# The first half of the tokens goes through all of stage B before the second half's output projection, and gets its u and z by seven block products

## The reference

```python
# mixer A
p = h @ w_in                                  # 1024 -> 3 x 1024
a, g_glu, z = split(p)
c = a * sigmoid(g_glu)
y = causal_dwconv(concat([hist, c]))          # 31 taps, channel by channel
y = silu(layernorm(y)) * silu(z)
x = x + rmsnorm(y @ w_out)                    # 1024 -> 1024
# mixer B
p = h @ w_in                                  # 1024 -> u, v, z of 2048 each
u, v = split(gelu(p[:2 * 2048])) ; z = p[2 * 2048:]
v = layernorm(v)
mixed = einsum('gij,bcjgd->bcigd', w_s, v) + bias   # w_s 128x128 for each group, block-causal
s = (u * mixed) * silu(z)
x = x + rmsnorm(s @ w_out)                    # 2048 -> 1024
```

## Time and profile before

| | |
|---|---|
| median of three runs | 2355.88 us (2352.59 to 2357.32) |
| the profiled execution | 2360.95 us, span 2359.2 us |
| TensorE's mean granted clock | 0.992 of full speed |
| busy: TensorE, VectorE, ScalarE, GpSimd | 98%, 64%, 36%, 10% of the span |
| bytes over the span | 265.20 MB, mean 112 GB/s |

### The profile page before, as it was taken

One profiled execution on the slowest core, in us unless ns is written; L12 is line 12 of the kernel. 1 busy time (PEld: TensorE's weight loads), 2 busy tenths in 40 slices (PEclk: granted clock), 3 DMA queues, 4 the chain that ended last, 5 costly groups with the idle time before them and its releaser, 6 DMA issues.

```text
span 2359.2 us, 29993 instructions
## 1 busy us (share of the span) xinstructions
PE 2303.3 (98%) x12208; PEld 2009.2 (85%) x12208; DVE 1507.5 (64%) x1913; ACT 845.5 (36%) x1329; POOL 243.8 (10%) x419
## 2 busy tenths in 40 slices
PE   7899999999999999999999999999999998999998
PEld 6788899999888888888877878879999997888885
DVE  5589889887578988888735852277766766222121
ACT  5422223223353214343544542226566665111110
POOL 1100000010221110000001211111000000100000
PEclk9999999999999999999999999999999999999999
DMA  4323333322544313333442442213333236232220
GB/s 164 124 89 100 106 118 136 109 102 92 166 165 166 114 69 94 106 114 104 141 153 98 144 153 94 83 45 93 103 98 101 96 102 243 107 107 98 82 93 23
DMA packets 118441, 265.20 MB, mean 112 GB/s; under 512 B 16288, under 2 KB 52384, under 8 KB 116256
## 3 DMA queue, kind: packets, MB, share of 16 engines
q1 hardware_dynamic: 94816, 184.64, 24.1%
q0 software_dynamic: 23488, 78.64, 8.8%
HBM read 184.86 MB, written 78.75 MB: 112 GB/s over the span
## 4 chain that ended last, share of the span: by engine, by line
PE 95%; DMA 1%; DVE 1%; ACT 1%; issue 1%; POOL 0%; SPq 0%; ACTq 0%; DVEq 0%
PE PS L1879 30%; PE PS L1880 30%; PE PS L1881 30%; PE PS L2083 1%; PE PS L2111 1%; PE PS L1925 1%; PE PS L1947 1%; PE PS L1890 1%; DMA raw<-wa_in_in 0%; DMA zb<-silu_z_scratch 0%; PE PS L1934 0%; DMA xt<-x_in 0%; DVE xn L1322 0%; PE PS L2113 0%; ACT xn L951 0%
## 5 line engine op out<-in xcount | busy, mean ns | idle before, releaser
L1351 DVE SCALAR_TENSOR_TENSOR acc<-cp,cw,acc 128x513 f32<-128x513 f32 (+3 forms) x464 | 360.4, 777 | 13.9
L1879 PE MATMUL PS<-HAh,Wh 128*128 128x512 f32 (+2 forms) x960 | 342.0, 356 | 0.1
L1880 PE MATMUL PS<-HAl,Wh 128*128 128x512 f32 (+2 forms) x960 | 340.1, 354 | 0.0
L1881 PE MATMUL PS<-HAh,Wl 128*128 128x512 f32 (+2 forms) x960 | 340.0, 354 | 0.0
L1879 PE MATMUL PS<-Wbh,s7h 128*128 128x512 f32 (+1 forms) x544 | 213.2, 392 | 8.0 <-issue 6.4
L1880 PE MATMUL PS<-Wbl,s7h 128*128 128x512 f32 (+1 forms) x544 | 212.9, 391 | 0.0
L1879 PE MATMUL PS<-Vh,HBh 128*128 128x512 f32 (+1 forms) x544 | 212.7, 391 | 0.1
L1881 PE MATMUL PS<-Wbh,s7l 128*128 128x512 f32 (+1 forms) x544 | 212.6, 391 | 0.0
L1880 PE MATMUL PS<-Vl,HBh 128*128 128x512 f32 (+1 forms) x544 | 212.1, 390 | 0.0
L1881 PE MATMUL PS<-Vh,HBl 128*128 128x512 f32 (+1 forms) x544 | 211.9, 390 | 0.0
L1879 PE MATMUL PS<-HBh,Uh 128*128 128x512 f32 x512 | 203.5, 398 | 0.8 <-ACT vb L1091 0.8
(11 more groups left out here) (223 smaller groups left out, 4715.6 us busy)
## 6 DMA issues: line engine op xcount, KB each, us to landing
raw<-wa_in_in SPq DMA_DIRECT2D x48, 512.0 KB, 3.5
rawv<-wb_v_in SPq DMA_DIRECT2D x64, 256.0 KB, 4.8
rawu<-wb_uz_in SPq DMA_DIRECT2D x32, 512.0 KB, 3.5
v_scratch<-vb POOLq DMA_DIRECT2D x64, 256.0 KB, 2.6
vt<-v_scratch SPq DMA_DIRECT2D x32, 512.0 KB, 3.7
s_scratch<-m POOLq DMA_DIRECT2D x32, 512.0 KB, 3.6
st<-s_scratch SPq DMA_DIRECT2D x16, 1024.0 KB, 4.8
xt<-x_in SPq DMA_DIRECT2D x16, 512.0 KB, 4.5
```

Of the source, the lines that this page charges most:

```text
L1351: return nc.vector.scalar_tensor_tensor(out=out, in0=src, scalar=w, in1=first, op0=ALU.mult, op1=ALU.add)
L1879: nc.tensor.matmul(out, wh, xh, start=start, stop=False, skip_group_check=seeded)
L1880: nc.tensor.matmul(out, wh, xl, start=False, stop=False, skip_group_check=seeded)
L1881: return nc.tensor.matmul(out, wl, xh, start=False, stop=stop, skip_group_check=seeded)
```

## The change

The order on every engine becomes: A; O, V, Q and B of the first half; then O, V, Q and B of the second half. The pieces:

- **U goes.** `q_stage` takes the half h as an argument, and for the first half each block column has one sub with 512 columns (`NG`, `GW`): 84 matmuls of 512 columns. The row sums of the mixing matrices are formed on TensorE between M2 and M7 of the first block column, in each half.
- **The weights' sums** T3, B11, T2, T1 and B21 lie in one array `QW` in order, and are split by one instruction for the first two and one for the other three.
- **The token sums of the first half**: S1, S2 and S3 are formed during V's last quarter, S4 only behind the row sums, at the start of Q (`s_add(h, "S4a")` to `"S4c"`, then `s_low(h, "S4")`).
- **B in two parts.** W is loaded and split once for each half. There are two buffers for s instead of three; the second tile comes in LAG = 10 rows after the first, and the first tile's s is loaded and split in two parts of EARLY = 14 and 2 rows.
- **The convolution**: 12 instead of 11 steps in the later units of A, none in V's last quarter, 3 instead of 6 in each third of a block column, and the last 88 steps in B: 20 at each of tiles 0 to 3 and 8 at tile 4, five ahead of a tile's split of s and the rest behind it.
- **The second half's first tiles**: the load of y of tile 8 stands in SyncE's program at tile 4 of the first half's B; its transposes stand on TensorE in tile 5, its spreading and the transposes of tiles 9 and 10 in tiles 6 and 7. The output weights of A for the second half are split in the last tile.

The diff, cut to this core (where functions were rewritten, only their new lines stand here, since the old ones are in the listing above):

```diff
-TH = WIDTH[1] // 2
-GW = TH // 2
+TH = tuple(w // 2 for w in WIDTH)
+NG = (1, 2)
+GW = tuple(t // n for t, n in zip(TH, NG))
+SUBS = tuple(KB * n for n in NG)
...
+SLOTS = ("T3", "B11", "T2", "T1", "B21")
+SPLITS = (slice(0, 2), slice(2, 5), "B22", "T4")
...
+EARLY, LAG = 14, 10
...
-    room = [(("A", n), 6 if n < 6 else 7 if n >= 44 else 11) for n in range(4, 2 * UNITS_A - 2)]
-    room += [(("V", q, i), 3 if q == 0 else 5) for q in range(NQ) for i in range(8)]
-    room += [(("U", j, part), n) for j in range(KB) for part, n in enumerate((6, 6, 6))]
+    room = [(("A", n), 6 if n < 6 else 7 if n >= 44 else 11 if n < 24 else 12) for n in range(4, 2 * UNITS_A - 2)]
+    room += [(("V", q, i), 3 if q == 0 else 5) for q in range(NQ - 1) for i in range(8)]
+    room += [(("U", j, part), 3) for j in range(KB) for part in range(3)]
+    room += [(("B", t), 20) for t in range(5)]
...
+        def quad_order(h):
+            last = SUBS[h] - 1
+            order = [(m, 0) for m in ("M1", "M6", "M2")] + [("rs", 0)] + [(m, 0) for m in ("M7", "M5")]
+            order += [("mix", 0)] * (NG[h] == 1)
+            for sub in range(1, last + 1):
                 order += [("M1", sub), ("M7", sub), ("M3", sub - 1), ("M4", sub - 1), ("M6", sub)]
...
+            def b_stage(h):
+                first, n = TILES[h][0], len(TILES[h])
+                s_load(first, 0)
+                for i in range(10):
+                    wb_load(h, i)
+                s_load(first, 1)
+                s_load(first + 1)
+                for i in range(10, KB):
+                    wb_load(h, i)
...
+                for i in range(n):
+                    if i + 2 < n:
+                        s_load(first + i + 2)
+                        b_load_x(first + i + 2)
+                    if h == 0:
+                        c_loads(("B", i))
+                    if h == 0 and i == 4:
                         o_load_y(8)
                         o_load_z(8)
                         o_load_y(9)
...
+            def q_stage(h):
...
+                u_sums(h)
+                if h == 0:
+                    for c in "abc":
+                        s_add(h, f"S4{c}")
+                s_low(h, "S4")
+                q_low(h, "B22", 0)
+                q_low(h, "T4", 0)
                 for j in range(KB):
                     if j > 0:
+                        p = q_last(h, j - 1)
+                        if h == 1:
+                            u_mixed(h, j - 1)
+                        add_22(h, p)
+                        q_add_up(h, "T1", j)
+                        q_add_up(h, "T4", j)
+                        if h == 0:
+                            u_mixed(h, j - 1)
+                        q_low(h, SPLITS[1], j)
+                        q_gate_u(h, 0, j - 1)
+                    fill(("U", j, 0) if h == 0 else None)
+                    if h == 0 and j + 1 < KB:
+                        q_add_up(h, "T3", j + 1)
+                    fill(("U", j, 1) if h == 0 else None)
+                    if j > 0:
+                        add_21(h, p)
+                        q_low(h, "B22", j)
+                        q_low(h, "T4", j)
+                    if h == 0:
+                        u_add_bias(h, j)
+                        if j + 1 < KB:
+                            q_add_up(h, "T2", j + 1)
+                            q_low(h, SPLITS[0], j + 1)
+                    if j > 0:
+                        q_gate_u(h, 1, j - 1)
+                        q_gate_z(h, j - 1)
+                    fill(("U", j, 2) if h == 0 else None)
...
+                            q_low(h, SPLITS[0], j + 1)
+                u_mixed(h, KB - 1)
+                add_22(h, last)
+                t_low(first, 0)
+                q_gate_u(h, 0, KB - 1)
+                b_low(h, 0)
+                b_low(h, 1)
+                add_21(h, last)
+                q_gate_u(h, 1, KB - 1)
...
+            def b_stage(h):
...
+                dve.wait_ge(b_g, 16 * (h + 1))
+                for i in range(n):
+                    t = first + i
+                    if h == 0 and i == n - 1:
+                        for k in range(KD):
+                            wo_low(1, k)
+                    b_gain(t)
+                    b_post_norm(t)
+                    k0, k1 = steps_at.get(("B", i), (0, 0)) if h == 0 else (0, 0)
+                    conv_steps(k0, min(k0 + 5, k1))
+                    if i + 2 < n:
+                        t_low(t + 2)
+                    conv_steps(min(k0 + 5, k1), k1)
...
+            def b_first_tiles(h):
+
+                first, last_sub = TILES[h][0], SUBS[h] - 1
                 steps = []
                 for i in range(KB):
+                    steps += [(first, i)] + [(first + 1, i - LAG)] * (i >= LAG)
+                steps += [(first + 1, i) for i in range(KB - LAG, KB)]
                 for t, i in steps:
+                    if t == first:
+                        pe.wait_ge(b_lo, KB * h + i + 1)
+                    if t == first and i == 0:
+                        pe.wait_ge(b_sl, b_split(t, 0))
+                        pe.wait_ge(u_gel, q_gel(h, "C11", last_sub))
+                        pe.wait_ge(q_add, q_added(h, "C21", last_sub - 1))
+                    if t == first and i == EARLY:
+                        pe.wait_ge(b_sl, b_split(t))
+                    if t == first + 1 and i == 0:
+                        pe.wait_ge(b_sl, b_split(t))
+                        pe.wait_ge(u_silu, q_silu(h, "C12", last_sub))
+                        pe.wait_ge(q_add, q_added(h, "C21", last_sub))
                     for c in range(2):
...
+            def b_stage(h):
+                first, n = TILES[h][0], len(TILES[h])
+                b_first_tiles(h)
+                for i in range(2, n):
+                    t = first + i
+                    pe.wait_ge(b_sl, b_split(t))
+                    if i == 2:
+                        pe.wait_ge(q_copy, q_copied(h, "m7", SUBS[h] - 1))
+                        pe.wait_ge(u_mev, KB * (h + 1))
+                    else:
+                        pe.wait_ge(o_pm, bi(t) - 2)
+                    if h == 0 and i == n - 1:
+                        b_last_tile(t)
+                        continue
+                    for c in range(2):
+                        for k in range(KB):
+                            last = b_row(t, k, c)
+
+                        if (h, i, c) == (0, 5, 0):
+                            o_transpose(8, 0)
+                        if (h, i, c) == (0, 5, 1):
+                            o_transpose(8, 1)
+                        if (h, i, c) == (0, 6, 0):
+                            o_spread(8)
+                            o_transpose(9, 0)
+                    last.then_inc(o_main, 1)
+
+            def b_last_tile(t):
+
+                for k in range(KB):
+                    for c in range(2):
+                        last = b_row(t, k, c)
+                    if k < KD:
+                        last.then_inc(b_left, 1)
+                    if k == 1:
+                        o_transpose(9, 1)
+                    if k == 4:
+                        o_spread(9)
+                        o_transpose(10, 0)
+                    if k == 9:
+                        o_transpose(10, 1)
                 last.then_inc(o_main, 1)
...
-            u_stage()
+            q_stage(0)
+            b_stage(0)
             o_stage(1)
             v_stage(1)
-            q_stage()
-            b_first_tiles()
-            for t in range(3, NTILES):
-                pe.wait_ge(b_sl, t + 1)
-                if t >= 4:
-                    pe.wait_ge(o_pm, b_tile(t) - 3)
-                b_tile_product(t)
+            q_stage(1)
+            b_stage(1)
 
 
```

1381 lines of the change are left out of this document (649 added, 732 removed).

## The result

The changed kernel takes 2366.26 us (median of 6 runs, 2365.39 to 2366.76) against 2355.93 (6 runs) for the one before: ratio 1.0043, 95% interval 1.003 to 1.0056. It is slower by 10.3 us, and its profiled span is longer by 5.8, where the sum had -8.3. The forecast of 2347.5 was wrong, and the time lies outside its range of 2330 to 2364.

What follows compares the result with a forecast made beforehand. TensorE was taken as the bound, busy 2303.3 of 2359.2 us. Terms -43.6 - 13.9 + 17.6 + 9.5 + 19.0 + 2.6 + 0.5 = -8.3 gave about 2347.5 us for the median; range 2330 to 2364.

Steps and rivals of the forecast that it cites:

- Part 1: First half's u and z: 84 instead of 96 matmuls in each of sixteen block columns, at 0.2269 us each: -43.6 us.
- Part 2: Old u and z stage, first half: its losses go as tile 8's transposes leave it: -13.9 us.
- Part 3: Start of the first half's products: TensorE waits 12.6 us for VectorE's split, plus short waits and clock: +17.6 us.
- Part 4: Start of the first half's stage B with two s buffers: waits at W's third and eleventh rows: +9.5 us.
- the forecast's remark on bandwidth: Start of stage B: W's rows want 385 GB/s, under the limit near 435, so nothing is added.
- Part 5: First half's stage B: 88 conv steps delay tile 8's y, TensorE waits 15.8 us in tile 5: +19.0 us.
- Part 6: Work done twice: row sums again 1.7, the second half's start 0.9: +2.6 us.
- Part 7: The rest: W loaded and split twice beside matmuls; second half's B starts as before with two buffers: +0.5 us.
- The third rival: Both starts of stage B lose 5 us more each, s or W coming late: +10, 2358 us; chance 0.16.
- y's wait was there: First rival denied it: VectorE's steps end before TensorE reaches tile 8's transpose, 18.4 us go: 2329; chance 0.17.
- the second rival: VectorE bounds the first half's sixteen rounds, 22.0 instead of 20.84 us each: +19, 2366 us; chance 0.15.
- the forecast's own signs: Mixing 20.8 to 20.9 us apart; waits of 12 to 13 and 14 to 17; VectorE's steps done about 97 after tile 0.

Runs made afterwards that it cites:

- e2_s4: Changed kernel with two of S4's additions ahead of the row sums, and T3, T2 and the two-slot split ahead of S4's low part: 2360.8 us, ratio 1.0011.
- e1_gelu: Changed kernel with ScalarE's split of stage B's first s moved behind the gelu, first half only: 2365.13 us, ratio 1.0031.
- e10_wlate: e1_gelu with the first rows of W for the first half's B loaded behind the last M3 instead of M5: 2367.17 us, measured once.
- e1_both: e1_gelu with `add_22` ahead of the mixed sum on VectorE in the first half: 2361.8 us, ratio 1.0015.
- e6_wfirst: e1_both with the low parts of s and of W's first two rows also ahead of the mixed sum: 2357.13 us, ratio 0.9997.
- e4_conv13: e1_both with thirteen instead of twelve conv steps a unit of stage A from unit 24 on: 2353.39 us, ratio 0.9979.
- e5_u444: e1_both with twelve instead of nine conv steps a block column in the first half's u and z: 2354.67 us, ratio 0.9983.
- e9_conv_u: Changed kernel with e6_wfirst's and e2_s4's orders, second tile 13 rows behind, ten or eleven conv steps a column but the first: 2325.73 us, ratio 0.9864.

## Why the prediction was wrong

*Part 1, the products: right.* 20.84 us a round was measured. The price by the pitch and not by the mean of a matmul's rows held. Two readings beside it are off and carry nothing: the mean in the earlier trace rows is 0.398 and not the 0.394 that was multiplied, and 0.127 to 0.129 for 272 columns is 5 to 7% above the same price by columns, which is 0.1205.

*Part 2, the losses of the old stage: right.* No wait for y's statistics is left ahead of B.

*Part 3, the start of the products: right.* +17.6 was forecast with a wait of 12.6. The changed kernel shows

```profile
910.38 0.79 PE L1943 MATMUL PS<-HBh,QW 128*128 128x512 f32 x1 [12.20 <-DVE QW L1360]
```

and matmuls 0.43 us apart behind it, in a stretch whose granted clock is 0.74 (910.3 to 920). Its short waits are 0.76 and 1.53, so 14.5 of the 18.0 that this start cost; the twelve matmuls at the lower clock level took 5.2 us instead of 2.7, and 1.0 is spread over the rest. VectorE's split of two slots came at 909.10 and 1.23 long, at the end of the very chain that was worked out. e2_s4 shows that the order of this chain was the cause.

*Part 4, the start of B: the step that failed.* What it priced came out near: +9.5 for the waits of the rows of W, measured 1.92, 0.73 and 5.76 and some 2.7 for the clock, 11.1. What it left out, a term put at nothing, is the end of u and z just ahead of it: 8.85 us before the last M3, and 2.5 for the clock, 11.4. Its sentence was "TensorE's third row of W waits about 3 us for VectorE, which still forms the last gates". It followed VectorE from the last product on, and not what stands in front of `add_22` while TensorE waits for it: the mixed sum, the store and ScalarE's split. The rows for it were there, the store of 3.6 us and the order of the instructions, but the forecast did not ask what the newly placed split of s waits for and what is queued behind it. e1_gelu, e10_wlate, e1_both and e6_wfirst show each link, and in e6_wfirst the stage is back at its forecast (352.8 for 353.1).

The part also took 3.6 us for a store. In the changed kernel the store of column 15, which the second tile's s waits for, landed after 8.2; the forecast's remark on bandwidth, "nothing is added", was written for the loads of W alone and did not ask what a store beside them would cost.

*Part 5, the wait for y: right.* 15.7 us measured, 15.8 forecast. The end of its chain, in order of time:

```profile
1381.34 0.81 DVE yc L1421
1382.15 0.29 issue
1382.44 0.90 POOL y_scratch L890
1383.35 3.18 DMA y_scratch<-yc
1386.52 0.02 issue
1386.54 3.17 DMA yb<-y_scratch
...
1389.76 1.11 PE PS L1989 x4
1390.87 0.43 PE PS L1943
```

From the end of tile 0's product (ScalarE's first read of it is at 1282.97) TensorE was at the transpose after 91.1 us, 91.3 worked out, and VectorE's last step ended after 99.2, 97.6 worked out. Both transfers were shorter than their medians (3.2 each for 4.1 and 4.4), which evened it out: that the 15.8 came so close is in part luck. e4_conv13, e5_u444 and e9_conv_u show that the 88 steps are the cause: with fewer of them in B the wait goes.

*Part 6: +3.8 for 2.6.* Near enough; no run takes it apart.

*Part 7, the second B: +5.2 for 0.5, mis-sized.* "As before with two buffers" was not so. TensorE's row after the changed kernel's second wait for W is

```profile
2170.80 0.79 PE L1943 MATMUL PS<-Wbh,s7h 128*128 128x512 f32 x1 [7.51 <-DVE Wbl L1360]
```

Waits there are 12.5 us in all, where the old start had 8.0. W's last six rows are split behind the second tile's s (SyncE loads it 14.5 us after the first row; before the change it left ahead of W). The reason is in the program: the old stage B began with tiles of the first half, whose s had been stored a stage before, so the load of its second tile waited only for M7; the new one begins with tiles 8 and 9, whose last block column is only just being stored. The third rival had this: both starts of B worse by 5 each. It was right in kind for the second half and gave 2358; that the first start would lose 11.4 at a third place was in no rival.

*The rivals.* y's wait was there. VectorE was not the bound of the rounds: the second rival's 2366 is the time measured, and not its reason, since the rounds stand at 20.84; e5_u444 shows where it begins. Nor did the forecast's own signs warn: the mixing at 20.84, the wait of 12.2 at 20 us into the stage, the 15.7 in tile 5 and VectorE's end at 99.2 for 97 all came as it said. None of them looked at the place between the two stages.

So the miss of 14.8 us between the last matmuls is +11.4 before M3, +4.7 in the second B, +0.9 in the first, +1.2 in part 6 and -3.4 in the stages that the sum left alone. That the profiled run of before lay 5 us over its median adds to it: the spans differ by 5.8, the medians by 10.3, and the forecast for the median was -8.4.

Left open: each half of the change by itself (the early B with eight products, the seven products in the old order) was not run, so that seven products pay is read from the pitch and not shown by a run. The rest of the waits for W in e9_conv_u, 17.9 us in both halves, was not taken on, nor the 3.3 us by which the stretch up to the first product differs between before and after, which is no more than traces of one and the same stage A differ.

## What to carry to other kernels

When a stage is put behind another one, follow each in-order queue through the seam and ask of every instruction that is put there: what does it wait for, and who stands behind it? The cost here was not the new stage's work but that its first split, its loads and its low parts stood ahead of, or beside, the last steps of the old one; five calls in another order gave 9 us back (e6_wfirst), and with the other starts and the share of conv steps mended too the change was worth 31 us and not -10. Price a product by the pitch between two like marks in the chain, and give the less busy engine as much filler a round as keeps it just under that pitch, not less and not more.

## What the runs showed of the hardware

- The same 512 KB store landed 3.4 us after its issue with no large load beside it (e10_wlate), and 8.1 with four loads of 512 KB issued on another queue at the same moment (e1_gelu); the four loads took 6.7 us there by the median, and 4.9 without the store. A median of landing times hides that.
- Each long gap costs twice: after gaps of 8.8, 12.2 and 15.7 us the matmuls stood 0.43 us apart for a while, at the lower clock level (1.2 GHz), and the granted clock of 910.3 to 920 was 0.74. Behind the first two, twelve matmuls took 5.2 us instead of 2.7, so 2.5 more each; behind the third, the longest, it was less: four transposes and the seven matmuls after them took 3.7 us, and the pitch was back at 0.23. For the third and the waits for W ahead of it together the stage lost 5.3 beyond the waits (29.4 - 15.7 - 8.4).
